# Head mixing of a hybrid RWKV-7 and window-attention block: the work on a head pair before its inversion moves into the inversion and the scan of the pair ahead of it

## What is computed

```python
z  = rmsnorm(x) @ w_in                     # project_in, stored transposed (zT)
zr = zr + (shifted(zr) - zr) * mu          # token shift
w  = -softplus(-(w0 + tanh(wd) @ w_up)) - 0.5 ;  decay = exp(-exp(w))
a  = sigmoid(a0 + ad @ a_up) ;  g = sigmoid(gd) @ g_up
kk = unit(k * k_k) ;  k = k * (1 + (a - 1) * k_a)
S_t = S_{t-1} diag(decay_t) + (S_{t-1} (-kk_t)) (kk_t a_t)^T + v_t k_t^T ;  y_t = S_t r_t     # per head of 64
y_rwkv = (groupnorm(y) * ln_g + ln_b + sum(r k r_k) v) * g
y_attn = chunked window attention with ALiBi and sinks, 16 heads
h = x + concat(y_rwkv, y_attn) @ w_out     # project_out
h = h + two experts of 32 (top-1 group, top-2 experts), SwiGLU     # route, experts
out = rmsnorm(h)                           # finish
```

## Time and profile before

| | us |
|---|---|
| median of 3 runs | 4069.07 (4030.44 to 4094.3) |
| the profiled execution | 4064.9 |
| its span | 4063.1 |
| the 8 turns, 931.8 to 2234.4 | 1302.6 |
| PE busy in the span | 3415.6 (84%) |
| mean granted TensorE clock | 0.869 of 2.4 GHz |

### The profile page before, as it was taken

One profiled execution on the slowest core, in us unless ns is written; L12 is line 12 of the kernel. 1 busy time (PEld: TensorE's weight loads), 2 busy tenths in 40 slices (PEclk: granted clock), 3 DMA queues, 4 the chain that ended last, 5 costly groups with the idle time before them and its releaser, 6 DMA issues. The chain is left out here.

```text
span 4063.1 us, 47176 instructions
## 1 busy us (share of the span) xinstructions
PE 3415.6 (84%) x16935; PEld 2826.9 (70%) x16935; DVE 1964.5 (48%) x2656; ACT 1568.2 (39%) x2031; POOL 312.3 (8%) x246
## 2 busy tenths in 40 slices
PE   6999999975786786968777799855999999999970
PEld 5888888864674674857657587754888888888860
DVE  3101010115545545253463222235888888888865
ACT  4111111103332332222232221124777777777751
POOL 0000000000000000000000000012111122111101
PEclk8999999986886876665777899967999999999985
DMA  3212121221101101000000532245999999999966
GB/s 130 78 62 77 62 77 62 77 70 38 40 18 33 40 18 33 18 28 23 22 24 9 223 134 93 68 145 203 372 379 381 379 376 376 378 379 384 384 244 260
DMA packets 169043, 629.47 MB, mean 155 GB/s; under 512 B 66116, under 2 KB 72516, under 8 KB 105604
## 3 DMA queue, kind: packets, MB, share of 16 engines
q1 hardware_dynamic: 159236, 595.01, 39.9%
q0 software_dynamic: 9728, 33.60, 2.1%
HBM read 582.17 MB, written 79.92 MB: 163 GB/s over the span
## 5 line engine op out<-in xcount | busy, mean ns | idle before, releaser
L1668 DVE TENSOR_TENSOR w_lo_e<-raw,w_hi_e 128x2048 fp32r<-128x2048 f32 x384 | 874.1, 2290 | 179.5 <-ACT w_hi_e L1607 179.4
L1607 ACT ACTIVATE w_hi_e<-raw 128x2048 fp32r<-128x2048 f32 x384 | 735.9, 1927 | 298.4 <-PE ps_y L1724 109.9
L236 PE MATMUL psA<-hn_hi,w_lo 128*128 128x512 f32 x1184 | 473.0, 399 | 0.0
L234 PE MATMUL psA<-hn_hi,w_hi 128*128 128x512 f32 x1184 | 465.0, 393 | 6.5 <-DVE w_lo L218 6.5
L235 PE MATMUL psA<-hn_lo,w_hi 128*128 128x512 f32 x1184 | 467.2, 395 | 0.0
L218 DVE TENSOR_TENSOR w_lo<-wraw,w_hi 128x2048 fp32r<-128x2048 f32 x37 | 84.8, 2293 | 710.5 <-ACT w_hi L193 710.5
L200 ACT ACTIVATE z_sb<-psA 128x512 f32<-128x512 f32 x74 | 44.3, 598 | 720.8 <-PE psA L236 720.8
L234 PEld LDWEIGHTS psA<-hn_hi,w_hi 128*128 128x128 f32 x1184 | 222.8, 188 | 60.1 <-DVE w_lo L218 6.7
L235 PEld LDWEIGHTS psA<-hn_lo,w_hi 128*128 128x128 f32 x1184 | 222.7, 188 | 57.9
L236 PEld LDWEIGHTS psA<-hn_hi,w_lo 128*128 128x128 f32 x1184 | 222.6, 188 | 51.2
L1219 PE MATMUL psD<-wo_hi,y_hi 128*128 128x512 f32 x512 | 201.4, 393 | 40.8 <-DVE wo_lo L1191 40.8
(11 more groups left out here) (310 smaller groups left out, 6081.5 us busy)
## 6 DMA issues: line engine op xcount, KB each, us to landing
raw<-in_w_gate SPq DMA_DIRECT2D x128, 1024.0 KB, 9.7
raw<-in_w_up SPq DMA_DIRECT2D x128, 1024.0 KB, 7.5
raw<-in_w_down SPq DMA_DIRECT2D x128, 1024.0 KB, 9.1
wraw<-in_w_in SPq DMA_DIRECT2D x37, 1024.0 KB, 5.4
wo_raw<-in_w_out SPq DMA_DIRECT2D x32, 1024.0 KB, 5.0
zT<-z_sb SPq DMA_DIRECT2D x36, 512.0 KB, 2.9
y<-yk SPq DMA_DIRECT2D x8, 2048.0 KB, 9.6
z<-zT SPq DMA_DIRECT2D x26, 512.0 KB, 4.5
```

Source lines behind the costliest of these rows:

```text
L234: nc.tensor.matmul(ps[2 * b + h][:, :], w_hi[:, b, k, :], hn_hi[:, k, cols], start=k == 0, stop=False)
L236: last = nc.tensor.matmul(ps[2 * b + h][:, :], w_lo[:, b, k, :], hn_hi[:, k, cols], start=False, stop=k == KT - 1)
L1607: nc.scalar.activation(hi[:, s, :], raw[:, r, :], ACT.Copy).then_inc(hi_set, 1)
L1668: nc.vector.tensor_tensor(lo[:, s, :], raw[:, r, :], hi[:, s, :].bitcast(F32), ALU.subtract).then_inc(lo_set, 1)
```

## The change

**Order.** The next pair n = turn + 1 is prepared inside turn `turn`. Its loads, shift, projections, key norm and bonus products stand in the gap of the inversion; the log decays, exponentials, keys and rates follow the three levels; its transposes and scores stand in the scan, two units per chunk, both in one PSUM bank (`SCORE_BANK = 4`), and the transposes in one bank (`NAT_BANK = 2`). The gate's matmuls are done at level 6 of their own turn. Group norm goes chunk by chunk inside the scan, with the output transposed two chunks later; the last two chunks' part falls into the gap of the next turn. `X` and `Y` have storage of their own. The common start of a turn is gone. The first pair's front, transposes and scores stand alone ahead of the loop; the first and last turn are written out and turns 1 to 6 are a loop. The attention slots have other places.

**Blocks.** Instead of 8 DMAs of 16x16 blocks there are 4 of 32x32 squares (`quarter`), with a scratch row of `DROW` = 528 elements; the DMA that fills `AD` and the one that writes `m_diag` now move 16 runs of 16 elements per partition (`corners`), where each moved one run of 256.

**Elsewhere.** `route` issues the experts' first six weight loads after the `xn` stores; `finish` has four `y2` buffers.

```diff
-        T_BANK, Y_BANK, X_BANK = (0, 1), (2, 3), (2, 4, 3, 4)
-        SCORE_BANK = (4, 2, 3, 0)
+        LORA_BANK, BONUS_BANK, WIDE_BANK, SUM_BANK, GATE_BANK = (1, 4, 2, 1), (2, 3), (2, 1), 4, 4
+        NAT_BANK, SCORE_BANK = 2, 4
-        PLACES = {"norm": (0,), "diag out": (1, 2), "diag back": (3,), "level 5": (4,), "chunk 0": (5,),
-                  "chunk 1": (6,), "chunk 2": (7,), "chunk 3": (8,), "chunk 5": (9,), "chunk 6": (10,), "chunk 7": (11,)}
+        PLACES = {"gap 0": (0,), "gap 1": (1,), "level 4": (2,), "level 5": (3,), "level 6": (4,), "chunk 0": (5,), "chunk 1": (6,),
+                  "chunk 2": (7,), "chunk 3": (8,), "chunk 4": (9,), "chunk 5": (10,), "chunk 6": (11,)}
...
                 def move_blocks(turn):
                     wait(sp, score_set, turn, UNITS)
-                    for b in range(NBB):
-                        at = slice(b * BB, (b + 1) * BB)
-                        sp.dma_start(a_diag[b].rearrange("u i j -> i u j"), SC[at, :, 0, at]).then_inc(diag_saved.sem, 16)
-                    wait(sp, diag_saved, turn, 16 * NBB)
-                    sp.dma_start(AD[:, 0:BB * BB], a_diag.rearrange("b u i j -> (b u) (i j)")).then_inc(diag_out.sem, 16)
+                    for b in range(QB):
+                        at = slice(b * QW, (b + 1) * QW)
+                        sp.dma_start(quarter(a_diag, b), SC[at, :, 0, at]).then_inc(diag_saved.sem, 16)
+                    wait(sp, diag_saved, turn, 16 * QB)
+                    sp.dma_start(AD[:, 0:BB * BB].rearrange("r (i c) -> r i c", c=BB), corners(a_diag)).then_inc(diag_out.sem, 16)
...
+                def body(turn, first=False, last=False):          # PE
+                    n = turn + 1
+                    if not first:
+                        flip_out(turn - 1, TT - 2)
+                    if not last:
+                        lora(n, 0, first)
+                        lora(n, 1)
+                    bonus(turn, first)
+                    attend(attend_pe, pe, turn, "gap 0")
+                    if not last:
+                        lora(n, 2)
+                        lora(n, 3)
...
+                    for j in range(TT):
+                        chunk(turn, j, last)
                         if j >= 2:
+                            flip_out(turn, j - 2)
+                        if not last:
+                            flip_nat(n, j)
+                            if j == 0:
+                                wait(pe, gated, turn, 2)
+                            scores(n, 2 * j)
+                        attend(attend_pe, pe, turn, f"chunk {j}")
+                        if not last:
+                            scores(n, 2 * j + 1)
...
+                    for j in range(TT):                           # DVE, in the scan
+                        if not last:
+                            row_operands(n, j)
+                        if j < TT - 1:
+                            wait(dve, s_done, turn, j + 1)
+                            wait(dve, s_set, turn, j + 1)
+                            nc.vector.scalar_tensor_tensor(Ss[:, (j + 1) % 2, :], ps_S, dec[:, j:j + 1], ones[:, :], ALU.mult, ALU.mult)\
+                                .then_inc(s_set.sem, 1)
+                        if j >= 2:
+                            normalise(turn, j - 2)
+                        if j:
+                            stats(turn, j - 1)
+                        if not last:
+                            mask_scores(n, 2 * j)
+                        attend(attend_dve, dve, turn, f"chunk {j}")
+                        if not last:
+                            mask_scores(n, 2 * j + 1)
...
-                for to, source, arrived in ahead:
-                    sp.dma_start(to, source).then_inc(arrived, 16)
                 for t in range(TT):
                     sp.wait_ge(xn_set, t + 1)
                     sp.dma_start(xn[t * P:(t + 1) * P, :], xt[:, t % 2, :]).then_inc(stored[t % 2], 16)
+                for to, source, arrived in ahead:
+                    sp.dma_start(to, source).then_inc(arrived, 16)
...
-        y2, o = sb("y2", [P, 2, TOPK, D]), sb("o_f", [P, 2, D])
+        YS = 4
+        y2, o = sb("y2", [P, YS, TOPK, D]), sb("o_f", [P, 2, D])
```

More of the change, by code:

```diff
@@ L532, in attend, with run @@
                 step(engine, turn, k)
+        def run(engine, body):
+            body(0, first=True)
+            with engine.Fori(1, PAIRS - 1) as turn:
+                body(turn)
+            body(PAIRS - 1, last=True)
         with nc.Block() as block:
@@ L702, in _ @@
-                    attend(attend_act, act, turn, "flip")
-                    wait(act, affine, turn, 2)
-                    act.sem_inc(turn_over, 1)
+                        nc.scalar.activation(Un[:, :], ps_U, ACT.Copy).then_inc(u_set.sem, 1)
+                        wait(act, out_done, turn, j + 1)
+                        nc.scalar.activation(ynat[:, tile(j)], ps_out, ACT.Copy).then_inc(out_set.sem, 1)
+                        if not last:
+                            copy_nat(turn + 1, j)
@@ new lines, in body @@
+                def body(turn, first=False, last=False):
+                    n = turn + 1
+                    if not last:
+                        parameters(n)
+                    if not first:
+                        normalise(turn - 1, TT - 2)
+                        stats(turn - 1, TT - 1)
+                    if not last:
+                        shift_in(n, 1, 0)
+                        keys(n)
+                        shift_in(n, 0, 1)
+                    if not first:
+                        normalise(turn - 1, TT - 1)
+                    bonus(turn, 0)
+                    if first:
+                        attend(attend_dve, dve, turn, "gap 0")
+                    else:
+                        dve.wait_ge(o_stored, 16 * turn)
+                        attend(attend_dve, dve, turn, "gap 0")
@@ L850, in _ @@
                     wait(dve, diag_out, turn, 16)
                     invert_blocks(dve, turn)
-                    attend(attend_dve, dve, turn, "diag back")
+                    if not last:
+                        norms(n)
+                    if not first:
+                        finish_half(turn - 1, 1)
+                    nc.vector.tensor_copy(lnx[:, :], here(turn, LNX_G, LNX_G + 2)).then_inc(lnx_set.sem, 1)
+                    bonus(turn, 1)
+                    if not last:
+                        spread_norms(n)
+                        shift_in(n, 2, 2)
+                        unit_keys(n)
@@ L853, in _ @@
+                    attend(attend_dve, dve, turn, "gap 1")
                     for lev in range(BASE, LEVELS):
@@ L913, in _ @@
-                    assert steps[0] == dve_step.per_turn, steps[0]
+                        if not last:
+                            mask_scores(n, 2 * j + 1)
+                    finish_half(turn, 0)
+                parameters(0)
+                shift_in(0, 1, 0)
+                keys(0)
+                shift_in(0, 0, 1)
+                norms(0)
+                spread_norms(0)
+                shift_in(0, 2, 2)
+                unit_keys(0)
+                log_decay(0, first=True)
+                centre(0)
@@ L1026, in _, with bonus @@
-                    attend(attend_pe, pe, turn, "diag out")
-                    attend(attend_pe, pe, turn, "diag back")
-                    wait(pe, diag_back, turn, 16 * NBB)
+                def bonus(turn, first):
+                    wait(pe, bonus_in, turn, 1)
+                    wait(pe, nat_set, turn, TT)
+                    if not first:
+                        wait(pe, affine, turn - 1, TT - 2)
+                    for i in range(2):
+                        mm(ps[BONUS_BANK[i]][:, :], ones[:, :], rrk[:, half(i)], start=True, stop=True).then_inc(bonus_done.sem, 1)
@@ new lines, in _ @@
+                for i in range(4):
+                    lora(0, i, first=True)
+                sums(0)
+                widen(0)
+                wait(pe, kk_set, 0, 2)
+                for j in range(TT):
+                    if j:
+                        wait(pe, nat_set, 0, j)
+                    flip_nat(0, j)
+                    scores(0, 2 * j)
+                    scores(0, 2 * j + 1)
+                run(pe, body)
+                for j in (TT - 2, TT - 1):
+                    flip_out(PAIRS - 1, j)
```

756 lines of the change are left out of this document (420 added, 336 removed).

## The result

The changed kernel took **3900.77 us** (median of 4 runs, 3884.79 to 3930.72) beside 4074.09 us of the kernel before: a ratio of 0.9618, 95% interval 0.9512 to 0.9723. The forecast was 3885, so it was 16 us too low and right in sign and size. The profiled execution took 3930.72 us (span 3928.9), the slowest of the four: 134.2 us less span than the profiled 4063.1 of before, where the forecast's sum had 185. Three lines of the page, for the lines in the earlier trace rows; the last counts DMA packets, of which 66116 were under 512 B before.

What follows compares the result with a forecast made beforehand. No engine is full: a turn is a chain of parts with different bounds, and TensorE's clock matters as much. 4064.9 - 187 (turns) + 30 (slow scan) - 28 (route, finish) = 3880, stated as 3885; 8 in 10 within 3785 to 4005.

Steps and rivals of the forecast that it cites:

- Removed: Each turn's front 29.3, transposes and scores 16.8 and tail 12.4 would run beside other work: 58.5 us off.
- First pair: Ahead of the loop: front alone 29.3 us, then 16 score units at about 2 us, 32; together 61.
- Gap: Block moves and inversion, 20.7 us before: DMAs +2.6 and DVE's later entry +2.4, so +5.0 a turn.
- Levels: Levels, 39.8 us before: more attention slot work and the gate's products (3.4) add 7.3; added DVE work costs nothing.
- rival (b): Head mixing: the clock stays high, levels gain 4 to 5 us a turn, no slow scan; 3800 us, chance 0.13.
- Scan: Scan, 37.6 us before: score units, transposes, waits for the norm and hand-overs add 25.6, to 63 us.
- Half a slow scan, +30: Scans: a slow scan at 1.2 GHz costs about 57 us more; half of one expected per execution, +30 us.
- Rival (e): PE drops to 1.2 GHz at the levels' end throughout the scan, 120 us each; six such give 4197, chance 0.07.
- rival (c): Hidden DVE work shows, 10 us a turn, in late masked copies, later inversion, longer chunks: 3955 us, chance 0.17.
- Rival (d): Next pair's operands miss the scan's start behind ACT's exponentials; about 20 us a turn given back: 4025, chance 0.08.
- Route: In route, weight loads behind the xn stores remove DVE's 21.77 us wait for the first store: -20 us.
- Finish: In finish, four y buffers remove DVE's waits for y in five tiles of eight: -8 us.

Runs made afterwards that it cites:

- second profile: The changed kernel profiled again with no edit, on another chip: 3897.37 us, ratio 0.9736, profiled span 3882.9 us.
- two-bank kernel: Changed kernel, but the first pair's 16 score units, ahead of the loop, alternate between two score banks: 3884.14 us, ratio 0.9687.
- filled gaps: Changed kernel plus six 128x512 products that nothing reads in the gap of turns 2 to 7: 3882.11 us, ratio 0.9669.
- last kernel: Changed kernel with output transpose later in the chunk, turns written out, two score banks for the first pair, six unread products in the gap: 3802.27 us, ratio 0.9473.
- later transpose: Changed kernel with chunk j-2's output transpose moved behind the next pair's operand transposes and first score unit: 3849.08 us.

## Why the prediction was right, and where its terms were not

| term, us | forecast | first profile | second profile |
|---|---|---|---|
| first pair alone | 61 | 90.0 | 90.2 |
| seven gaps | 7 x 25.7 = 180 | 207.0 | 206.1 |
| seven levels | 7 x 47.1 = 330 | 279.0 | 273.0 |
| seven scans, with the clock's 30 | 7 x 63.2 + 30 = 472 | 510.6 | 464.8 |
| last turn and end | 109 + 9 = 118 | 109.7 | 118.9 |
| head mixing | 1146 | 1196.3 | 1153.0 |
| route, finish | -28 | -18.9 | -24.3 |

(The forecast's column adds up to 1161; the text took 15 off, since turn 4, whose parts these are, was 2.1 longer than the mean turn without its slow clock.) The 134.2 us between the two first profiles are 106.3 in the turns, 6.1 ahead of them (the first pair's loads, which before stood outside the turns and now inside), 10.1 in route, 8.8 in finish and 3.0 less wait for the first `y`. In the second profile head mixing came within 7 us of the forecast, but by errors that cancel; that the total came within 16 is in part luck.

**Removed, 58.5 a turn: right.** Front, score part and tail run beside levels and scan: DVE has 23.8 of 37 us in the levels where it had 6.75 of 39.8, and no masked copy is late there.

**First pair, 61 forecast, 90.0 measured: the worst step.** 16 units "at about 2 us" took 3.0, 48.9 in all, since PE ran at 0.52 and a unit's products then take 1.7, as the forecast's own price list said. The two-bank kernel confirms the chain. The other 41.1 stand against a front of 29.3: 6.1 are the loads, and about 6 the first unit's operands, transposes and products, since the front's 29.3 ended before them. The kernel before needed 36.5 in its own first turn from 931.8 to its first masked copy; from the same point the changed one needs 35.0.

**Gap, +5.0 forecast, +10 measured in the steady turns: right in kind, wrong in cause.** The DMAs cost next to nothing: `AD` landed 3.0 us after issue instead of 2.0, not 5, and the four stores issued in 1.93 instead of 3.77. As a single DMA 2048 pieces of 64 bytes cost 1.0 us more than 128 of 1 KB on the way to `AD` and 1.3 more on the way to `m_diag` (3.0 instead of 1.7). The rule on pieces under 512 bytes (the Trainium skill, DMA: Bandwidth & Descriptors, Specifications), with which the forecast put the time at 3925, did not decide anything here. Instead DVE enters the inversion 8.2 us later, not 2.4, of which 2.6 is the loop's restart and 3.5 waits for PE's passes at the low clock. And behind the inversion the chain of norms ends the gap. I counted that DVE work, but not the PE and POOL steps between its parts: sums 2.27, widening 3.78, POOL's power 3.30.

**Levels, +7.3 forecast, -2.8 measured** (37.0 at 1.00; the mean of seven is 39.9). The added work was counted rightly, but the 39.8 it was added to ran at a mean of 0.75: that is 29.9 at 1.00 (an estimate from that row), and 7.3 more make 37.2. The levels run at 1.00 from the first transpose in four turns of seven, and 37.0 holds everything. That PE's work just ahead of them does this is argued, and the filled gaps speak for it: with them ten levels of twelve start at 1.00, without them five of twelve. This is rival (b)'s mechanism, priced there at 4 to 5 us a turn and worth 7 on average. In turns where the clock rose late they took 40.3 to 50.0.

**Scan, 63 forecast, 64.1 at the high clock: right.** The wait of PE for `gn` was charged 4.8 and is 3.9, where the forecast put it. Chunks with two units and a slot take 7.9 to 8.8 at 1.00. DVE's 34 us of work in it are 34.1.

**The clock.** "Half a slow scan, +30" was paid in another coin: no scan ran at 0.50 as a whole, but in the first profile the last two chunks of six scans did, 10 us each, and in the second those of one. Over 7 x 64.1 the scans took 62 us more in the first profile and 16 in the second, 39 on average. Rival (e)'s slow scans never came; that this is owed to the gate's wide products, as the forecast argued, no run tests. Of rival (c) the later inversion came, 8.2 us instead of 4, but the kernel with the inversion first shows that it does not set the gap; no masked copy was late in the levels. Rival (d) did not: no first right side waited for ACT.

**Route, -20 forecast, -10.1 measured in the first profile and -15.8 in the second**: the wait fell from 21.77 to 5.68 and 3.50, and what came back is the clock of PE, which paces the tiles behind it (0.80 before, 0.70 and 0.76 now). The forecast had no term for that. **Finish, -8 forecast, -8.8 and -8.5 measured**: right.

Open: why the clock falls in chunk 5 in one execution and at the scan's end in another. Pauses are not needed for it: in the last kernel it fell in four scans after PE had been busy without one for at least 8 us, in turn 5 for the 46.8 us of the scan up to there. What the windows do show is how long the stretch at 1.00 through levels and scan lasted: 72 to 96 us in the changed kernel's first profile (85 in three turns of seven), 85 to 102 in its second (96 in five), 85 in those four turns of the last kernel. Levels and scan together need 101 us at 1.00, with the later transpose 97, so a stretch of 85 ends inside the scan in both. What makes it 85 in one turn and 96 in another, no run separates. More work there moved the fall in most scans and not in all; that the later transpose gains more than its wait is measured, but what of it is the shorter scan and what the missing pauses was not taken apart.

## What to carry to other kernels

Price what will stand alone ahead of a pipeline as one chain up to its last result, and at the clock that PE has while it waits between the steps: here 0.52, and 3.0 us a unit instead of 2. When work is moved beside a wait, follow the whole chain through every engine that touches it, since the wait's place is taken by the longest of them and the engine named first (here DVE and the blocks) may not be it. Before a part's old time is used as a base, read the granted clock in it, and before an edit is judged by the part that it speeds up, read the parts behind it.

## What the runs showed that I had not expected

Products whose result nothing reads made the gap shorter: six where PE stood still raised the granted clock there from 0.57 to 0.83 and took 2.6 us off each gap. In the profiles the scans behind gave that back, and the medians, 15 and 17 us lower, are little against the spread. Nor did a clock that stood at 1.00 stay there: it fell after 85 us in scans in which PE had not paused. A wait of 0.5 us that stood in six chunks of each scan cost 27 us in plain time, and the kernel without it has a median about 50 us lower. And two profiles of the same program differed by 46 us, nearly all of it in where TensorE's clock fell and rose.
